# Gate and up weights of 26 experts by one 8 MB transfer each, in place of two of 4 MB

## The chip, the core and the metric

The kernel runs on one core of one Trainium2 chip. The metric is the device time of one execution in microseconds (us). The version before takes 1148.26 us (median of 3 runs, 1148.26 to 1148.38). One of its executions was profiled; the profile gives times in us from the span's start. TensorE (PE) does the matmuls, VectorE (DVE), ScalarE (ACT) and GpSimd (POOL) the rest, and SyncE (SP) issues nearly all transfers.

## The reference

One encoder layer for 256 tokens of width 1024: a token mixer, cross-attention into 256 memory tokens, then a routed feed-forward part with 32 experts. The last part is what the change touches:

```
logits = x2 @ w_router + b_router            # 256 x 32; each token takes its top 4 experts
gates  = softmax(top_vals)
h = x2[tok] @ w_gu[e] + b_gu[e]              # w_gu[e]: 1024 x 2048 f32, 8 MB: gate half, up half
g = min(h[:, :1024], 7);  u = clip(h[:, 1024:], -7, 7)
y = (u + 1) * (g * sigmoid(1.702 * g))
y @ w_down[e] + b_down[e]                    # w_down[e]: 1024 x 1024 f32, 4 MB
out = sum of gate * y over the token's 4 experts, then x <- LayerNorm(alpha * x + out)
```

Every token chooses its own experts, so every expert has some tokens, and all 32 x 12 MB of weights are read once.

## The kernel before

**Order of the experts.** The router counts the tokens of each expert. Experts are processed one after another in an order that the program computes (RANK_AT interleaves experts with many and with few tokens). I number them by this order: place 0 to place 31. A turn (UNROLL = 2) is an even place and the odd one behind it; there are 16 turns (LOOPS).

**Passes.** A pass handles up to 32 tokens (SLOTS) of one expert: gate and up in four chunks of 2 MB (64 matmuls on PE, line 1005), the scatter of the pass before (L981), transposes, the gather of the next tokens (L968), and down in two chunks (32 matmuls, L1030). An expert with more than 32 tokens takes several passes over the same weights. Places 1 and 25 are run by `two_passes`, which uses each chunk for two passes in turn, so that its four passes are two double ones; all others are run by `expert_pass`.

**Slots and transfers.** The weights lie in `ring`, 12 slots of 2 MB (16 KB in each of 128 partitions). Each of the two experts of a turn has six slots, in three units of two adjacent slots: unit 0 holds chunks 0 and 1 of gate and up, unit 1 chunks 2 and 3, unit 2 down. `load_later` runs on SP: for each unit it waits on `chunk_used` until PE has used both chunks for the last time, then issues one 4 MB transfer for the expert two places on. So place n + 2 is loaded while PE is at places n and n + 1, and the load of place n + 2's first unit is issued in the last pass of place n. All weights go through one queue in order. Places 0 to 3 are loaded in pieces of 2 MB, and so is most of place 31.

**What PE waits for.** In `expert_pass`, `chunk(c)` waits at every even chunk for the semaphores of its unit (`slot_landed`, `unit_landed`): at chunk 0 for unit 0, at chunk 2 for unit 1, and at the first chunk of down for unit 2.

Of the kernel before, what the change touches and what calls it, by code (L numbers as in the profile page):

```python
# [13 lines left out]
P = 128  # L14


D = 1024
# [15 lines left out]
N_EXP = 32  # L33
# [38 lines left out]
FILL_ORDER = [(0, 2), (0, 0), (0, 1), (0, 4), (0, 5), (0, 3), (1, 1), (1, 2), (1, 0), (1, 4), (1, 5), (1, 3)]  # L72

# [14 lines left out]
def layer_program(nc, x, memT, x_kv, w_mq, w_in, conv_p, early, early_par, late, w_out, ln_p, ln2_cols, w_cq, w_ck, w_cv, w_co,  # L88
                  w_router, b_router, w_gu, b_gu, w_down, b_down, out):
    with ExitStack() as ctx:  # L90
# [34 lines left out]
        lnp = S11[:, half:SLOT]  # L125
        ln3p = S6[:, 0:2 * D]
        normal_rows, rstd_last = S6[:, 2 * D:3 * D], S6[:, 3 * D:3 * D + P]
        aqT = qbuf[:, 0:1024].rearrange("p (m t) -> p m t", m=4)
# [278 lines left out]
        def _(sp):  # L407
# [22 lines left out]
            def load_piece_of_expert(e, c):  # L430
                src = w_gu[e, c // 2] if c < 4 else w_down[e]
                landed = unit_landed[e * UNITS_PER_EXPERT + c // 2] if c % 2 else slot_landed[chunk_slot(e, c)]
                sp.dma_start(slot_words(chunk_slot(e, c)), src[:, (c % 2) * SLOT:(c % 2) * SLOT + SLOT]).then_inc(landed, 16)

            def load_unit(e, u, i):
                at = UNIT_SLOT[u * UNITS_PER_EXPERT + i] * SLOT
                src = w_gu[bass.ds(e, 1), i].rearrange("o p n -> (o p) n") if i < 2 else w_down[bass.ds(e, 1)].rearrange("o p n -> (o p) n")
# [26 lines left out]
            def load_last_pieces(e, i, used):  # L464
                at = UNIT_SLOT[UNITS_PER_EXPERT + i]
                src = w_gu[bass.ds(e, 1), i].rearrange("o p n -> (o p) n") if i < 2 else w_down[bass.ds(e, 1)].rearrange("o p n -> (o p) n")
# [12 lines left out]
            def load_later(e0, ending=False):  # L479
# [12 lines left out]

            def load_in_pieces(e, u, i, used):
                at = UNIT_SLOT[u * UNITS_PER_EXPERT + i]
                src = w_gu[bass.ds(e, 1), i].rearrange("o p n -> (o p) n") if i < 2 else w_down[bass.ds(e, 1)].rearrange("o p n -> (o p) n")
                for h in range(2):
# [105 lines left out]
        def _(pe):  # L602
# [441 lines left out]

            def expert_pass(it, u, loads, ending=False, opening=False):
                j = pe.snap(passes, min_val=0, max_val=MAX_PASSES)

                def chunk(c):
                    s = chunk_slot(u, c)
                    if ending and c >= 2:  # L1050
                        if c % 2 == 0:
                            pe.wait_ge(slot_landed[s], 16 * (front_loads[s] + 3))
                        else:
                            pe.wait_ge(unit_landed[u * UNITS_PER_EXPERT + c // 2], it * 16 + 16)
                        return slot_words(s)
                    if c % 2 == 0:
                        pe.wait_ge(slot_landed[s], 16 * (front_loads[s] + loads))
                        pe.wait_ge(unit_landed[u * UNITS_PER_EXPERT + c // 2], it * 16 + 16)
                    return slot_words(s)
# [50 lines left out]

            def two_passes(it, u, loads):
                j = pe.snap(passes, min_val=0, max_val=MAX_PASSES)

                def chunk(c):
                    s = chunk_slot(u, c)
                    if c % 2 == 0:
                        pe.wait_ge(slot_landed[s], 16 * (front_loads[s] + loads))
                        pe.wait_ge(unit_landed[u * UNITS_PER_EXPERT + c // 2], it * 16 + 16)
                    return slot_words(s)
# [55 lines left out]

            def all_passes(it, u, ending=False):
                with pe.Fori(0, passes_at(bass.ds(it * UNROLL + u, 1))):
                    expert_pass(it, u, 2, ending)

# [5 lines left out]
            heavy_turn = HEAVY_AT // UNROLL  # L1185
            with pe.Fori(1, heavy_turn) as it:
                for u in range(UNROLL):
                    all_passes(it, u)
            for u in range(UNROLL):
                if u == HEAVY_AT % UNROLL:  # L1190
                    with pe.Fori(0, passes_at(slice(HEAVY_AT, HEAVY_AT + 1), 2), 2):
                        two_passes(heavy_turn, u, 2)
                else:
                    all_passes(heavy_turn, u)
            with pe.Fori(heavy_turn + 1, LOOPS - 2) as it:
                for u in range(UNROLL):
                    all_passes(it, u)
            pe.wait_ge(shift_landed, 16 * GROUPS)
# [3 lines left out]
            for u in range(UNROLL):  # L1202
                all_passes(LOOPS - 2, u)
            for u in range(UNROLL):
                if u == UNROLL - 1:
                    for t in range(TT):
                        for d in range(2):
                            add_rows(t, d)
                all_passes(LOOPS - 1, u, ending=u == UNROLL - 1)
            total = pe.snap(passes, min_val=1, max_val=MAX_PASSES)  # L1210
# [971 lines left out]
```

## Time and profile before

| | |
|---|---|
| median of 3 runs | 1148.26 us |
| the profiled execution | 1146.75 us, span 1144.8 us |
| PE busy | 1059.2 us (93% of the span) |
| DVE, ACT, POOL busy | 442.3, 153.9, 59.9 us |
| moved | 444.87 MB, mean 389 GB/s |
| transfers of 4 MB | 55 of gate and up, 27 of down |

PE is shown busy for 93% of the span, but a matmul counts as busy at half clock too, and between the experts PE also has waits for weights. The digits of part 2 of the page give the state in 40 equal slices of 28.6 us. The first 240 us are the mixer and the attention, the experts run from 247 us on, and the last 12 us are the final normalisation and the stores.

### The profile page before, as it was taken

The page shows a single profiled execution, that of the slowest core. Times are in us where ns is not written, and L with a number is a line of the kernel's source. Part 1 is how long each engine was busy: PE and PEld are TensorE (multiplying, and loading weights), DVE is VectorE, ACT ScalarE, POOL GpSimd, SP SyncE. Part 2 cuts the span into 40 slices and gives each one's busy share as a digit, 9 for nine tenths or more (in the row PEclk, how much of TensorE's full clock was granted, in tenths as well). Part 3 has the DMA queues.
Part 4 walks back from the last instruction along what each step waited for, and adds up shares of the span by engine and source line. Part 5 has one row for each costly group of instructions (what it writes and reads, how often), then busy time and mean ns, then how long its engine had stood idle before and what let it go on. Part 6 is the DMA issues. An engine that isn't in the chain of part 4 may idle for free.

```text
span 1144.8 us, 20191 instructions
## 1 busy us (share of the span) xinstructions
PE 1059.2 (93%) x8037; PEld 465.0 (41%) x8039; DVE 442.3 (39%) x1311; ACT 153.9 (13%) x334; POOL 59.9 (5%) x38
## 2 busy tenths in 40 slices
PE   9999999998999669999976669999979989999997
PEld 8876559543333213333321213333323333343333
DVE  2767577572533213333321113333313323333324
ACT  2142111230111001111100001111101101111101
POOL 0503370000000000000000000000000000000000
PEclk9999999999999889999987879999999999999999
DMA  9965356989999999999999999999999999999996
GB/s 331 365 233 184 110 189 253 379 324 428 423 433 428 437 430 432 432 429 434 428 437 430 432 433 428 434 428 437 429 433 434 427 433 426 436 428 429 433 425 248
DMA packets 36105, 444.87 MB, mean 389 GB/s; under 512 B 3876, under 2 KB 5160, under 8 KB 21256
## 3 DMA queue, kind: packets, MB, share of 16 engines
q1 hardware_dynamic: 33320, 439.86, 91.2%
q10 hardware_dynamic: 2752, 4.54, 1.3%
q8 instruction: 25, 0.41, 0.1%
q14 instruction: 8, 0.07, 0.0%
HBM read 443.34 MB, written 1.05 MB: 388 GB/s over the span
## 4 chain that ended last, share of the span: by engine, by line
PE 70%; DMA 23%; DVE 3%; another core or an unknown queue 2%; ACT 1%; issue 1%; DVEq 0%; SPq 0%; POOL 0%; POOLq 0%
PE bank L1005 23%; DMA ring<-in_w_down 15%; PE bank L1030 13%; DMA ring<-in_w_gu 8%; PE bank L689 6%; PE bank L981 6%; PE bank L635 5%; PE bank L968 3%; PE bank L814 2%; PE bank L877 2%; PE bank L974 2%; PE bank L1012 1%; PE bank L1018 1%; PE bank L1023 1%; PE bank L999 1%
## 5 line engine op out<-in xcount | busy, mean ns | idle before, releaser
L1005 PE MATMUL bank<-ring,wk 128*32 128x512 f32 x3072 | 369.9, 632 | 63.4 <-DMA ring<-in_w_gu 63.3
L1005 PEld LDWEIGHTS bank<-ring,wk 128*32 128x32 f32 x3072 | 103.9, 116 | 302.4 <-issue 263.8
L1030 PE MATMUL bank<-ring,wk 128*32 128x512 f32 x1632 | 204.8, 600 | 6.2 <-DMA ring<-in_w_down 6.2
L2036 DVE TENSOR_SCALAR wk<-bank 128x256 f32<-128x256 f32 x51 | 21.6, 423 | 461.3 <-PE bank L1005 460.5
L981 PE MATMUL bank<-wk 64*128 64x512 f32 x416 | 103.3, 615 | 2.9 <-ACT wk L1436 2.9
L1030 PEld LDWEIGHTS bank<-ring,wk 128*32 128x32 f32 x1632 | 62.8, 110 | 74.7 <-issue 46.8
L1424 ACT ACTIVATE wk<-wk 128x256 f32<-128x256 f32 x51 | 21.2, 417 | 455.0 <-DVE wk L2036 455.0
L635 PE MATMUL bank<-ring 128*128 128x256 f32 x320 | 70.7, 381 | 0.0
L689 PE MATMUL bank<-ring 128*128 128x512 f32 x152 | 66.4, 593 | 0.0
L981 PEld LDWEIGHTS bank<-wk 64*128 64x128 f32 x416 | 35.8, 186 | 71.4 <-issue 64.0
L635 PEld LDWEIGHTS bank<-ring 128*128 128x128 f32 x320 | 60.2, 190 | 8.9 <-issue 0.8
L968 PE MATMUL bank<-res,wk 128*32 128x256 f32 x832 | 55.7, 385 | 1.5 <-DVE wk L1986 1.4
L1436 ACT ACTIVATE wk<-bank 128x512 f32<-128x512 f32 x51 | 30.4, 597 | 190.5 <-PE bank L1030 190.2
L1894 DVE TENSOR_TENSOR wk<-bank,sm 128x256 f32<-128x256 f32 x49 | 20.8, 424 | 66.7 <-PE bank L974 66.7
L689 PEld LDWEIGHTS bank<-ring 128*128 128x128 f32 x152 | 28.6, 190 | 34.3 <-issue 34.1
L2045 DVE COPY wk<-bank 128x256 f32<-128x256 f32 x51 | 21.7, 425 | 37.4 <-PE bank L1018 37.4
L1993 DVE TENSOR_REDUCE wk<-wk 128x32 f32<-128x128 f32 x104 | 34.5, 373 | 1.8
L974 PEld LDWEIGHTS bank<-late_c,wk 128*128 128x128 f32 x104 | 16.4, 206 | 43.2 <-issue 41.9
L1986 DVE TENSOR_REDUCE wk<-wk 128x32 f32<-128x128 f32 x102 | 33.4, 369 | 0.0
L1428 ACT ACTIVATE wk<-bank 128x256 f32<-128x256 f32 x51 | 19.6, 383 | 90.7 <-PE bank L1012 90.7
L968 PEld LDWEIGHTS bank<-res,wk 128*32 128x32 f32 x832 | 22.4, 109 | 18.5 <-DVE wk L1986 2.9
L1432 ACT ACTIVATE wk<-bank 128x256 f32<-128x256 f32 x51 | 19.5, 383 | 51.4 <-PE bank L968 51.4
(369 smaller groups left out, 881.4 us busy)
## 6 DMA issues: line engine op xcount, KB each, us to landing
ring<-in_w_gu SPq DMA_DIRECT2D x55, 4096.0 KB, 34.8
ring<-in_w_down SPq DMA_DIRECT2D x27, 4096.0 KB, 38.4
ring<-in_w_gu SPq DMA_DIRECT2D x18, 2048.0 KB, 13.4
ring<-in_w_down SPq DMA_DIRECT2D x9, 2048.0 KB, 11.8
ring<-in_w_in SPq DMA_DIRECT2D x4, 2048.0 KB, 19.3
ring<-in_w_ck SPq DMA_DIRECT2D x2, 2048.0 KB, 21.7
ring<-in_w_cv SPq DMA_DIRECT2D x2, 2048.0 KB, 18.0
ring<-in_w_cq SPq DMA_DIRECT2D x2, 2048.0 KB, 8.3
```

The costliest lines, as they stand in the source:

```text
L635: ins = mm(banks[m // 2][:, (m % 2) * 256:(m % 2) * 256 + 256], cols, rhs[:, k, :], start=k == 0, stop=k == KT - 1)
L689: ins = mm(bank[:], rows[:, k, :], cols[:, k, :], start=fresh and k == 0, stop=k == KT // 2 - 1, skip_group_check=True)
L814: ins = mm(bank[:, m * P:(m + 1) * P], cols[:, k, m * P:(m + 1) * P], rows[:, k, :], start=fresh and m == 0 and k == 0, stop=k == KT // 2 ...
L877: ins = mm(bank[:], rows[k], cols[:, k, :], start=fresh and k == 0, stop=k == KT // 2 - 1, skip_group_check=True)
L968: ins = mm(strip(6, g)[:, 0:Q], hot[:, t, :], res[:, t, Q * g:Q * g + Q], start=t == 0, stop=t == 1, skip_group_check=True)
L974: ins = nc.tensor.transpose(psum[5][:, b * P:(b + 1) * P], xrows.rearrange("p (q b) -> p b q", b=2)[:, b, :], ident)
L981: ins = mm(psum[2 * t + d][:], scatT[r, t * P:(t + 1) * P], ysb[r, :], start=False, stop=end, skip_group_check=True)
L1005: ins = mm(hidden(bank, g), rows[:, kk, c, :], half_columns(w[:, kk, :], g), start=False, stop=2 * c + kk == KT - 1, skip_group_check=True)
L1030: ins = mm(strip(7, 2 * d + b), actT[:, b, 2 * c + gg, :], wd[:, gg, b, 512 * d:512 * d + 512], start=c == 0 and gg == 0 and b == 1, stop= ...
L1436: af(ysb, psum[7][:], ACT.Copy).then_inc(y_ready, 1)
L1986: ins = v.reduce_sum(hot[:, t, :], eq[:, t].rearrange("p k s -> p s k"), AX_X)
L1993: ins = v.reduce_sum(hotg1[:, t, :], eq[:, t].rearrange("p k s -> p s k"), AX_X)
```

## The change

- The gate and up weights of one expert now lie in DRAM with 64 KB in one row per partition, where there were two blocks of 32 KB per partition, and the four slots of an expert's gate and up are adjacent (for even places unit 0 and unit 1 change slots: 4 to 7, where unit 0 had 6 and 7 and unit 1 had 4 and 5).
- For places 4 to 29 (turns 2 to 14, WHOLE_TURNS) SP waits until all four chunks of gate and up are used, and issues one transfer of 8 MB. Down still goes by one of 4 MB.
- PE waits at chunk 0 of these places for the 8 MB, and no longer at chunk 2. Places 0 to 3, 30 and 31 keep their smaller transfers.
- The last turn's counts of unit 1's semaphore start 13 lower (`after`), since that semaphore isn't used in whole turns, and turn 1 of PE is written out ahead of the loop.

```
+WHOLE_TURNS = range(2, LOOPS - 1)
-UNIT_SLOT = [6, 4, 0, 8, 10, 2]
+UNIT_SLOT = [4, 6, 0, 8, 10, 2]
...
+            def load_whole_gate_and_up(e, u, used):
+                at = UNIT_SLOT[u * UNITS_PER_EXPERT] * SLOT
+                for c in range(4):
+                    sp.wait_ge(chunk_used[c], used)
+                sp.nop(nofuse=True)
+                sp.dma_start(ring[:, at:at + 4 * SLOT], w_gu[bass.ds(e, 1)].rearrange("o p n -> (o p) n")).then_inc(unit_landed[u * UNITS_PER_EXPERT], 16)
...
                 for u in range(UNROLL):
-                    for i in range(UNITS_PER_EXPERT):
+                    if whole:
+                        load_whole_gate_and_up(experts[u], u, passes_till[u])
+                    for i in range(2 if whole else 0, UNITS_PER_EXPERT):
...
             with sp.Fori(2, LOOPS - 1) as it:
-                load_later(it * UNROLL)
+                load_later(it * UNROLL, whole=True)
...
-                    if c % 2 == 0:
+                    if c % 2 == 0 and not (whole and c == 2):
                         pe.wait_ge(slot_landed[s], 16 * (front_loads[s] + loads))
-                        pe.wait_ge(unit_landed[u * UNITS_PER_EXPERT + c // 2], it * 16 + 16)
+                        pe.wait_ge(unit_landed[u * UNITS_PER_EXPERT + c // 2], own * 16 + 16)
```

On SP, the loop over turns 2 to 14, for the even place of a turn, before:

```order
L482 TENSOR_LOAD wk
L482 ISA x2
L438 ISA [waits chunk_used0,chunk_used1]
L438 DMA ring<-in_w_gu 128x8192
L438 ISA [waits chunk_used2,chunk_used3]
L438 DMA ring<-in_w_gu 128x8192
L438 ISA [waits chunk_used4,chunk_used5]
L438 DMA ring<-in_w_down 128x8192
```

and after the change:

```order
L491 TENSOR_LOAD wk
L491 ISA x2
L447 ISA [waits chunk_used3,chunk_used2,chunk_used0,chunk_used1]
L447 DMA ring<-in_w_gu 128x16384
L440 ISA [waits chunk_used4,chunk_used5]
L440 DMA ring<-in_w_down 128x8192
```

The first transfer of gate and up moves from behind the use of chunk 1 to behind the use of chunk 3.

On PE, the double pass of place 25 (`two_passes`), from the first chunk of gate and up to the end of the fourth; unit_landed3 and unit_landed4 are its units 0 and 1. Before:

```order
L1005 MATMUL bank<-ring,wk 32x512 [waits unit_landed3,slot_landed8]
L1005 MATMUL bank<-ring,wk 32x512 x7
...
L1005 MATMUL bank<-ring,sm 32x512 [waits xg_ready]
L1005 MATMUL bank<-ring,sm 32x512 x7
...
L1005 MATMUL bank<-ring,wk 32x512 x8
L1005 MATMUL bank<-ring,sm 32x512 x8
L1005 MATMUL bank<-ring,wk 32x512 [waits unit_landed4,slot_landed10]
L1005 MATMUL bank<-ring,wk 32x512 x7
```

and after:

```order
L1016 MATMUL bank<-ring,wk 32x512 [waits unit_landed3,slot_landed8]
L1016 MATMUL bank<-ring,wk 32x512 x7
...
L1016 MATMUL bank<-ring,sm 32x512 [waits xg_ready]
L1016 MATMUL bank<-ring,sm 32x512 x7
...
L1016 MATMUL bank<-ring,wk 32x512 x8
L1016 MATMUL bank<-ring,sm 32x512 x8
```

The order of the matmuls stays. The wait for the second half of the weights is gone from the third chunk, and unit_landed3, ahead of the first, now stands for all four chunks.

## Rows read from the trace of the kernel before

**Rows 1.** Page, part 2: DMA share in tenths and GB/s in 40 slices.

```profile
DMA  9965356989999999999999999999999999999996
GB/s 331 365 233 184 110 189 253 379 324 428 423 433 428 437 430 432 432 429 434 428 437 430 432 433 428 434 428 437 429 433 434 427 433 426 436 428 429 433 425 248
```

**Rows 2.** Waits of PE: line, waited for, us in total, times, longest.

```profile
PE bank L1005 <- DMA ring<-in_w_gu: 63.3, 17, 5.2
PE bank L1030 <- DMA ring<-in_w_down: 6.2, 9, 1.0
```

**Rows 3.** Chain of waits, gate and up in places 7, 9, 16, 22: start, us, what.

```profile
419.61 5.34 PE bank L1005 x32
...
433.75 6.87 PE bank L1005 x64
...
478.23 6.87 PE bank L1005 x64
...
493.05 6.87 PE bank L1005 x64
...
695.99 6.87 PE bank L1005 x64
...
870.83 6.87 PE bank L1005 x64
```

**Rows 4.** Timeline of SP: first issue's start, us to the second's end.

```profile
452.23 3.77 SPq L438 DMA_DIRECT2D ring<-in_w_gu  x2
...
511.54 3.77 SPq L438 DMA_DIRECT2D ring<-in_w_gu  x2
...
803.42 3.77 SPq L438 DMA_DIRECT2D ring<-in_w_gu  x2
...
889.33 3.76 SPq L438 DMA_DIRECT2D ring<-in_w_gu  x2
...
977.72 7.20 SPq L438 DMA_DIRECT2D ring<-in_w_gu  x2
```

**Rows 5.** Landing of in_w_down issued at 404.62, 478.25, 770.13, 844.27, 930.13, in turn.

```profile
DMA to landing us min/median/max: 53.7/53.7/53.7
...
DMA to landing us min/median/max: 38.4/38.4/38.4
...
DMA to landing us min/median/max: 37.9/37.9/37.9
...
DMA to landing us min/median/max: 51.1/51.1/51.1
...
DMA to landing us min/median/max: 54.2/54.2/54.2
```

**Rows 6.** Timeline of PE: start, us, engine, line, operation, idle before and releaser.

```profile
380.67 6.53 PE L1005 MATMUL bank<-ring,wk 128*32 128x512 f32 x32 [4.68 <-DMA ring<-in_w_gu]
...
390.47 5.04 PE L1005 MATMUL bank<-ring,wk 128*32 128x512 f32 x32 [3.28 <-DMA ring<-in_w_gu]
...
681.85 6.12 PE L1005 MATMUL bank<-ring,wk 128*32 128x512 f32 x32 [3.90 <-DMA ring<-in_w_gu]
...
856.69 5.34 PE L1005 MATMUL bank<-ring,wk 128*32 128x512 f32 x32 [4.46 <-DMA ring<-in_w_gu]
...
934.38 1.92 PE L1005 MATMUL bank<-ring,wk 128*32 128x512 f32 x16 [2.94 <-DMA ring<-in_w_gu]
...
953.80 3.64 PE L1030 MATMUL bank<-ring,wk 128*32 128x512 f32 x32 [0.20 <-DMA ring<-in_w_down]
...
1130.27 1.07 PE L1030 MATMUL bank<-ring,wk 128*32 128x512 f32 x8 [1.03 <-DMA ring<-in_w_down]
```

**Rows 7.** Landings: in_w_gu issued at 1080.49 (4 MB), in_w_down at 1089.39 (2 MB).

```profile
DMA to landing us min/median/max: 30.1/30.1/30.1
...
DMA to landing us min/median/max: 35.9/35.9/35.9
```

**Rows 8.** Page, part 6: issues, KB each, median us to landing.

```profile
out<-res SPq DMA_DIRECT2D x2, 256.0 KB, 2.4
```

More of the change, by code:

```diff
@@ L430, in load_piece_of_expert @@
             def load_piece_of_expert(e, c):
-                src = w_gu[e, c // 2] if c < 4 else w_down[e]
+                src = w_gu[e, :, (c // 2) * 2 * SLOT:(c // 2) * 2 * SLOT + 2 * SLOT] if c < 4 else w_down[e]
                 landed = unit_landed[e * UNITS_PER_EXPERT + c // 2] if c % 2 else slot_landed[chunk_slot(e, c)]
@@ L465, in load_last_pieces @@
                 at = UNIT_SLOT[UNITS_PER_EXPERT + i]
-                src = w_gu[bass.ds(e, 1), i].rearrange("o p n -> (o p) n") if i < 2 else w_down[bass.ds(e, 1)].rearrange("o p n -> (o p) n")
+                src = w_gu[bass.ds(e, 1)].rearrange("o p n -> (o p) n")[:, i * 2 * SLOT:i * 2 * SLOT + 2 * SLOT] if i < 2 else w_down[bass.ds(e, 1)].rearrange("o p n -> (o p) n")
                 sp.wait_ge(chunk_used[2 * i], used)
@@ L477, in load_last_pieces, with load_later @@
                     sp.dma_start(slot_words(at + 1)[:, half:SLOT], src[:, SLOT + half:2 * SLOT]).then_inc(done, 16)
-            def load_later(e0, ending=False):
+            def load_later(e0, ending=False, whole=False):
                 passes_till = [sp.value_load(cum_i[0:1, bass.ds(e0 + (u - UNROLL), 1)], min_val=1, max_val=MAX_PASSES) for u in range(UNROLL)]
@@ L494, in load_in_pieces @@
                 at = UNIT_SLOT[u * UNITS_PER_EXPERT + i]
-                src = w_gu[bass.ds(e, 1), i].rearrange("o p n -> (o p) n") if i < 2 else w_down[bass.ds(e, 1)].rearrange("o p n -> (o p) n")
+                src = w_gu[bass.ds(e, 1)].rearrange("o p n -> (o p) n")[:, i * 2 * SLOT:i * 2 * SLOT + 2 * SLOT] if i < 2 else w_down[bass.ds(e, 1)].rearrange("o p n -> (o p) n")
                 for h in range(2):
@@ L1043, in _, with expert_pass @@
             open_sum(1, 1)
-            def expert_pass(it, u, loads, ending=False, opening=False):
+            def expert_pass(it, u, loads, ending=False, opening=False, whole=False, after=0):
                 j = pe.snap(passes, min_val=0, max_val=MAX_PASSES)
@@ L1049, in chunk @@
                     s = chunk_slot(u, c)
+                    own = it - after if c // 2 == 1 else it
                     if ending and c >= 2:
@@ L1109, in expert_pass, with two_passes @@
                 pe.reg_add(passes, passes, 1)
-            def two_passes(it, u, loads):
+            def two_passes(it, u, loads, whole=False, after=0):
                 j = pe.snap(passes, min_val=0, max_val=MAX_PASSES)
@@ L1115, in chunk @@
                     s = chunk_slot(u, c)
-                    if c % 2 == 0:
+                    if c % 2 == 0 and not (whole and c == 2):
+                        own = it - after if c == 2 else it
                         pe.wait_ge(slot_landed[s], 16 * (front_loads[s] + loads))
-                        pe.wait_ge(unit_landed[u * UNITS_PER_EXPERT + c // 2], it * 16 + 16)
+                        pe.wait_ge(unit_landed[u * UNITS_PER_EXPERT + c // 2], own * 16 + 16)
                     return slot_words(s)
@@ L1174, in passes_at, with all_passes @@
                 return pe.value_load(npass_i[0:1, place], min_val=least, max_val=SEQ // SLOTS)
-            def all_passes(it, u, ending=False):
+            def all_passes(it, u, ending=False, whole=False, after=0):
                 with pe.Fori(0, passes_at(bass.ds(it * UNROLL + u, 1))):
-                    expert_pass(it, u, 2, ending)
+                    expert_pass(it, u, 2, ending, whole=whole, after=after)
             with pe.Fori(0, passes_of_first):
@@ L1185, in _ @@
             heavy_turn = HEAVY_AT // UNROLL
-            with pe.Fori(1, heavy_turn) as it:
+            for u in range(UNROLL):
+                all_passes(1, u)
+            with pe.Fori(2, heavy_turn) as it:
                 for u in range(UNROLL):
-                    all_passes(it, u)
+                    all_passes(it, u, whole=True)
             for u in range(UNROLL):
@@ L1191, in _ @@
                     with pe.Fori(0, passes_at(slice(HEAVY_AT, HEAVY_AT + 1), 2), 2):
-                        two_passes(heavy_turn, u, 2)
+                        two_passes(heavy_turn, u, 2, whole=True)
                 else:
-                    all_passes(heavy_turn, u)
+                    all_passes(heavy_turn, u, whole=True)
             with pe.Fori(heavy_turn + 1, LOOPS - 2) as it:
                 for u in range(UNROLL):
-                    all_passes(it, u)
+                    all_passes(it, u, whole=True)
             pe.wait_ge(shift_landed, 16 * GROUPS)
@@ L1202, in _ @@
             for u in range(UNROLL):
-                all_passes(LOOPS - 2, u)
+                all_passes(LOOPS - 2, u, whole=True)
             for u in range(UNROLL):
@@ L1208, in _ @@
                             add_rows(t, d)
-                all_passes(LOOPS - 1, u, ending=u == UNROLL - 1)
+                all_passes(LOOPS - 1, u, ending=u == UNROLL - 1, after=len(WHOLE_TURNS))
             total = pe.snap(passes, min_val=1, max_val=MAX_PASSES)
```

13 lines of the change are left out of this document (7 added, 6 removed).

## The prediction

> **What bounds the kernel now.** I read four views, in this order. The slices of the page first [rows 1]: from the tenth on, the DMA engines show a busy share of nine tenths or more in every slice, at 423 to 437 GB/s, up to the last. The waits of PE next [rows 2]: 17 waits for gate and up weights, 63.3 us in all, 9 for down weights, 6.2 us. Both say that from about 260 us on the weight stream is the resource. Then the end: the last down piece is waited for 1.03 us, at 1130.27 [rows 6], and only the closing stage follows. So the end is the end of the stream, and the stream's end is its work plus every gap in which its queue is empty. In the kernel before there is no such gap. Last, how close it comes to one: for each expert I compare the time at which SP issues a load with the time at which the transfer ahead of it in the queue lands.
>
> Six units of 4 MB lie between the landings of two down units, 404.62 + 53.7 = 458.3 and 478.25 + 38.4 = 516.6 [rows 5]: 9.72 us each, 431 GB/s.
>
> The queue is shortest where SP has waited for an expert of three or four passes. There the first gate and up unit is issued at 452.23 (place 7), 511.54 (place 9), 803.42 (place 19), 889.33 (place 22) and 977.72 (place 25, the double one) [rows 4], and the unit ahead lands at 458.3, 516.6, 808.0, 895.4 and 984.3 [rows 5]. That leaves 6.1, 5.1, 4.6, 6.1 and 6.6 us. Everywhere else in places 4 to 29 the timeline and the landings leave clearly more, or the load isn't merged.
>
> **What the change takes from this slack.** It acts twice.
>
> *The issue comes later.* SP issues at the use of chunk 3, where it issued at that of chunk 1. That is where the second issue of each pair stands now: the pairs end 3.77 us after the first one's start (7.20 us at place 25, where every chunk serves two passes) [rows 4], so at 456.0, 515.3, 807.2, 893.1 and 984.9. On SP only the down load stands behind the wait, which is later anyway. By itself this leaves room everywhere but at place 25, where 984.9 is past 984.3.
>
> *The pass starts later.* PE now waits at chunk 0 for all 8 MB. Where it runs ahead of the stream, it starts a place when the second half lands: at 419.61 rather than 9.8 us before in place 7. The first two chunks, which were computed while the second half came in, now lie behind it. An ordinary pass takes 493.05 - 478.23 = 14.82 us from start to start [rows 3]. From 419.61 the next would start at 434.43 + e, against 433.75 now: 0.7 us + e late. Places 16 (681.85, next 695.99) and 22 (856.69, next 870.83) give the same 0.7 + e [rows 3, 6]. So most of the 9.7 us is hidden, because down used to be waited for in that pass; it lands before PE gets there now.
>
> e is the price of the clock. After waits of 3.3 to 4.7 us PE ran the next 32 matmuls in 5.04, 5.34, 6.12 and 6.53 us [rows 6] against 6.87 / 2 = 3.43 at full clock [rows 3]: 1.6, 1.9, 2.7 and 3.1 more, since the granted clock was the lower of its two levels (1.2 GHz against 2.4) for part of them. The idle time ahead of these passes will be some 12 us (29.2 us for 12 MB less a pass and e), which no row shows; I take the mean of the four, e = 2.3, between 1.6 and 3.1.
>
> At place 25 nothing hides it. There chunks 0 and 1 are used for two passes, with transposes and the scatter between, from 934.38, and the down wait of 0.20 us ends at 953.80 [rows 6], so PE needs 19.2 us from chunk 0 to down. Starting 9.72 us later, at 944.1, it reaches down at 963.3 + e: 9.5 + e late instead of 0.7 + e.
>
> *A start takes time.* After an empty queue the data doesn't flow at once. A store of 256 KB takes 2.4 us from issue to landing [rows 8], of which 0.6 are data at 431 GB/s, so start and completion together are at most 1.8. Counted from the end of the issue I take 1.2, between 0 and 1.8; it is no more than the row allows.
>
> **The gaps**, each as the end of the issue now + lateness + 1.2 - landing ahead:
> - place 7: 456.0 + 0.7 + e + 1.2 - 458.3 = e - 0.4 = 1.9 us
> - place 9: PE is still as late as after place 7 (it never waits in between), 515.3 + 0.7 + e + 1.2 - 516.6 = e + 0.6 = 2.9 us. This counts from the old stream, so it contains place 7's 1.9.
> - Behind it PE waits for weights again from place 13 on, so stream and PE are late alike.
> - place 19, lateness from place 16: 807.2 + 0.7 + e + 1.2 - 808.0 = e + 1.1 = 3.4 us
> - place 22: 893.1 + 0.7 + e + 1.2 - 895.4 = e - 0.4 = 1.9 us
> - place 25: 984.9 + 9.5 + e + 1.2 - 984.3 = e + 11.3 = 13.6 us
>
> Together 12.6 + 4e = 21.8 us. Place 28 has only the issue of place 30 behind it, which isn't merged, and PE finds its weights late by as much as the stream; nothing there. The PE waits that grow in places 5, 6 and 12 to 15 cost nothing, since the queue reaches past them.
>
> **What it gives back.** Larger transfers carry a smaller fixed share. Between the landing at 1080.49 + 30.1 = 1110.6 and that at 1089.39 + 35.9 = 1125.3 [rows 7] three pieces of 2 MB came in, 4.9 us each, or 9.8 for 4 MB against 9.72. So doubling a row's length saves about 0.08 us per pair. I take the same for the next doubling: 26 x 0.08 = 2.1 us, between 0 (if the chip cuts the 64 KB rows in two) and, for the rounding of these landings, 4. The slots' new order, the later use of slot 5 at the start, the wait instructions and the written-out turn are covered by the stream's slack: nothing.
>
> The Trainium skill, "DMA: Bandwidth & Descriptors", sections "Anatomy of one DMA" and "Rules for kernel authors", speaks for the change: a transfer costs 2.0 us and its bytes at 436 GB/s (for those issued from GpSimd), and small ones are to be coalesced. By that fit 4 MB take 11.6 us, and an estimate of 26 x 2.0 = 52 us would be given back. The trace doesn't agree: 9.72 us per 4 MB, as the next transfer already stands in the queue. By the rows the saving is 2.1.
>
> **Sum.** 21.8 - 2.1 = +19.7 us. On the profiled execution the span goes from 1144.8 to 1164.5, its time from 1146.75 to 1166.5; the median of the runs shown is 1.5 above that, so 1168.0 us.
>
> **The rivals.**
> 1. *Only the later issue counts, PE's late start is absorbed.* This ends on the other side, as no change. For it: at places 7, 16 and 22 all but 0.7 us of the 9.7 is hidden behind the down wait, if e is nothing. It would need PE to reach down at place 25 with the weights' landing too. Gaps then: place 9 516.5 - 516.6 = 0, place 19 808.4 - 808.0 = 0.4, place 25 986.1 - 984.3 = 1.8; 2.2 - 2.1 = +0.1, 1148.4 us. Against it: 19.2 us of work stand between chunk 0 and down at place 25. It turns where the lateness at place 25 is under 2 us. Chance 0.07.
> 2. *Larger transfers win.* The slack is more than I read, since a load starts the moment that it is issued and the queue never runs dry, and the fixed share goes: -2.1 us, 1146.2 (up to -4). Against: issue times on PE's side, which the rows have to a tenth. Chance 0.04.
> 3. *Only the double place makes a gap.* If the clock returns at once (e = 0) and a load starts in 0.3 us, places 7, 19 and 22 lose next to nothing and place 25 loses 11: about +9, 1157 us. Chance 0.10.
> 4. *Worse.* The clock stays low through a whole pass (e = 6.9 at the four places, 12.6 + 27.5 - 2.1): +38, 1186 us; or rows of 64 KB flow worse, at 424 rather than 431 GB/s for 218 MB: +9 more, 1177. For it: idle times of 12 us, which the trace never shows. Against: the lower clock ends within 6.5 us of work in each row. Chance 0.08.
>
> The forecast has 0.71. With e from 1.6 to 3.1, the start from 0 to 1.8 and the saving from 0 to 4 it lies between 12.6 + 6.4 - 4.8 - 4 = +10.2 and 12.6 + 12.4 + 2.4 - 0 = +27.4 us, 1158.5 and 1175.7 (the start changes four gaps). The ends that need all of them at once are unlikely, so the range 1157 to 1175 holds the forecast and half of rival 3, and leaves out rivals 1, 2 and 4. A measurement can tell 0.2%, 2.3 us, from no change: rival 2's 2.1 us stays within it, but its 4 does not, so I split its chance. Faster 0.02, same 0.09 (rival 1 and the rest of rival 2), slower 0.89.
>
> **What would show it.** The DMA share dips after places 7 or 9, 19, 22, and for over 10 us after 25; DMA idles between the issue and the unit ahead there. PE starts place 7 near 419.6 and its second pass near 436.7; the second pass pair of place 25 is some 12 us late beside the stream. PE's waits for in_w_gu are half as many but longer, and those for in_w_down go from the merged places. The rate of the full stretches stays 431 to 433 GB/s. I am wrong if the share stays full behind place 25, or if PE reaches down there no later than its weights.

## The result, and the profile after

| | before | after |
|---|---|---|
| median of 5 runs each, on one chip | 1148.26 us (1147.39 to 1149.21) | 1176.36 us (1173.58 to 1177.99) |
| profiled execution, span | 1146.75, 1144.8 us | 1175.41, 1173.6 us |
| PE busy | 1059.2 us | 1046.2 us |
| moved | 444.87 MB | 444.90 MB |

The change makes the kernel slower: 1.0243 times the time before (95% interval 1.0232 to 1.0254), 28.1 us. The forecast was 1168.0 us, with a range up to 1175. The direction and five of the six places were right; the time is 1.4 us outside the range, and 0.7 above the 1175.7 that the prediction got by adding up all its bounds.

Part 2 of the page, which answers to [rows 1] (a slice is 29.3 us now; PEclk is the granted clock in tenths):

```profile
PEclk9999999999999779999977879999979979998999
DMA  9965366799999999999999999998999998699996
GB/s 329 371 206 179 108 244 258 304 402 427 423 439 432 433 429 380 429 427 431 429 429 429 429 431 438 447 436 355 431 429 393 429 430 358 271 437 427 403 427 255
```

The stream no longer runs through. Dips stand in slice 16 (380 GB/s), 28 (355), 31 (393), 34 and 35 (358, 271) and 38 (403). Every other slice from the tenth to the 39th keeps 423 GB/s or more, as before. So the transfers aren't slower; the stream pauses. Five of the six pauses in the table below lie in these slices. The sixth, at place 9, is too short to show in its slice (the 18th, 427) and is read from the landings.

The waits of PE, which answer to [rows 2]:

```profile
PE bank L1016 <- DMA ring<-in_w_gu: 111.2, 10, 13.9
```

Ten waits instead of 17, but 111.2 us instead of 63.3, and none for down (6.2 us before).

The gaps, as in the prediction, are read from three things: SP's issues [rows 4], the landing of the down unit ahead [rows 5], and the landing of the load itself. SP's timeline:

```profile
459.35 0.33 SPq L447 DMA_DIRECT2D ring<-in_w_gu  x1
...
518.66 0.33 SPq L447 DMA_DIRECT2D ring<-in_w_gu  x1
...
814.35 0.33 SPq L447 DMA_DIRECT2D ring<-in_w_gu  x1
...
903.93 0.33 SPq L447 DMA_DIRECT2D ring<-in_w_gu  x1
...
1008.01 0.33 SPq L447 DMA_DIRECT2D ring<-in_w_gu  x1
...
1096.81 3.77 SPq L440 DMA_DIRECT2D ring<-in_w_gu  x2
```

From issue to landing of the down units ahead of them, issued at 407.47, 481.86, 777.54, 851.63, 941.28 and 1051.23:

```profile
DMA to landing us min/median/max: 51.4/51.4/51.4
...
DMA to landing us min/median/max: 38.0/38.0/38.0
...
DMA to landing us min/median/max: 34.4/34.4/34.4
...
DMA to landing us min/median/max: 52.6/52.6/52.6
...
DMA to landing us min/median/max: 53.6/53.6/53.6
...
DMA to landing us min/median/max: 47.8/47.8/47.8
```

And from issue to landing of the loads themselves (the last line is the pair of 4 MB for place 30, its first the minimum):

```profile
DMA to landing us min/median/max: 21.8/21.8/21.8
...
DMA to landing us min/median/max: 22.0/22.0/22.0
...
DMA to landing us min/median/max: 22.1/22.1/22.1
...
DMA to landing us min/median/max: 21.9/21.9/21.9
...
DMA to landing us min/median/max: 23.0/23.0/23.0
...
DMA to landing us min/median/max: 12.8/15.9/19.0
```

Where the queue is full, 8 MB take 19.35 us from landing to landing and 4 MB 9.71 (medians; a few loads land later, the one issued at 911.57 by 1.2 us). What the distance of two landings has beyond that is lost. A place stands for the load that is issued when PE has used that place's weights. Times in us:

| place | down ahead lands | issue ends, beyond that: forecast, measured | start: forecast, measured | lost: forecast, measured |
|---|---|---|---|---|
| 7 | 458.9 | 0.7, 0.8 | 1.2, 2.1 | 1.9, 2.9 |
| 9 | 519.9 | -0.2, -0.9 | 1.2, 2.3 | 1.0, 1.4 |
| 19 | 811.9 | 2.2, 2.8 | 1.2, 2.4 | 3.4, 5.2 |
| 22 | 904.2 | 0.7, 0.0 | 1.2, 2.2 | 1.9, 2.3 |
| 25 | 994.9 | 12.4, 13.4 | 1.2, 3.3 | 13.6, 16.8 |
| 28 | 1099.0 | none, -1.9 | none, 2.8 | 0, 0.9 |
| sum | | 15.8, 16.2 (places 7 to 25) | 6.0, 12.3 | 21.8, 29.5 |

(Place 9's forecast is what it adds to place 7's. The sums are of unrounded values. The start is the lost time less the column before it: for place 19, 814.35 + 22.1 = 836.45, less 811.9 is 24.55; less 19.35 it is 5.2, of which 2.8 are the late issue.) The lateness of the issues came out almost as forecast, 16.2 against 15.8. What is off is the start: 12.3 us against 6.0.

PE's timeline, gate and up of places 6, 7, 16, 22, 25 (the number in brackets is the idle time ahead, with its releaser):

```profile
391.06 8.43 PE L1016 MATMUL bank<-ring,wk 128*32 128x512 f32 x64 [13.58 <-DMA ring<-in_w_gu]
...
420.12 9.25 PE L1016 MATMUL bank<-ring,wk 128*32 128x512 f32 x64 [12.68 <-DMA ring<-in_w_gu]
...
686.00 9.43 PE L1016 MATMUL bank<-ring,wk 128*32 128x512 f32 x64 [12.50 <-DMA ring<-in_w_gu]
...
865.54 8.41 PE L1016 MATMUL bank<-ring,wk 128*32 128x512 f32 x64 [13.92 <-DMA ring<-in_w_gu]
...
956.18 3.64 PE L1016 MATMUL bank<-ring,wk 128*32 128x512 f32 x16 [13.60 <-DMA ring<-in_w_gu]
...
977.02 3.71 PE L1041 MATMUL bank<-ring,wk 128*32 128x512 f32 x32
```

The place starts when the whole 8 MB are in. In place 25 the down piece is reached 20.8 us after chunk 0 and waits for nothing: it landed long before.

### The profile page after: what moved, and what is told of

It is laid out like the page before. It is cut to its first block, busy times and chain, and to the rows that moved or that the text cites. A ratio compares the mean times of both kernels' runs of the same rounds, so it can differ in the third digit from the quotient of the medians.

```text
span 1173.6 us, 20065 instructions
## 1 busy us (share of the span) xinstructions
PE 1046.2 (89%) x8037; PEld 463.9 (40%) x8039; DVE 442.8 (38%) x1311; ACT 154.2 (13%) x334; POOL 60.1 (5%) x38
## 2 busy tenths in 40 slices
DMA packets 32363, 444.90 MB, mean 379 GB/s; under 512 B 3460, under 2 KB 4744, under 8 KB 20840
## 4 chain that ended last, share of the span: by engine, by line
PE 72%; DMA 22%; DVE 3%; another core or an unknown queue 1%; ACT 1%; issue 1%; DVEq 0%; SPq 0%; POOL 0%; POOLq 0%
PE bank L1016 26%; DMA ring<-in_w_gu 22%; PE bank L1041 11%; PE bank L700 6%; PE bank L992 6%; PE bank L646 5%; PE bank L979 3%; PE bank L825 2%; PE bank L888 2%; PE bank L985 1%; PE bank L1023 1%; PE bank L1029 1%; PE bank L1034 1%; PE bank L1010 1%; PE bank L856 1%
## 5 line engine op out<-in xcount | busy, mean ns | idle before, releaser
L1016 PE MATMUL bank<-ring,wk 128*32 128x512 f32 x3072 | 358.2, 617 | 111.2 <-DMA ring<-in_w_gu 111.2
L1041 PE MATMUL bank<-ring,wk 128*32 128x512 f32 x1632 | 206.0, 599 | 0.0
L1909 DVE TENSOR_TENSOR wk<-bank,sm 128x256 f32<-128x256 f32 x49 | 20.8, 425 | 60.0 <-PE bank L985 59.9
L1443 ACT ACTIVATE wk<-bank 128x256 f32<-128x256 f32 x51 | 19.6, 384 | 103.1 <-PE bank L1023 103.1
L985 PE MATMUL bank<-late_c,wk 128*128 128x128 f32 x104 | 26.4, 336 | 0.0
```

The costliest lines, as they stand in the source:

```text
L985: ins = nc.tensor.transpose(psum[5][:, b * P:(b + 1) * P], xrows.rearrange("p (q b) -> p b q", b=2)[:, b, :], ident)
L1016: ins = mm(hidden(bank, g), rows[:, kk, c, :], half_columns(w[:, kk, :], g), start=False, stop=2 * c + kk == KT - 1, skip_group_check=True)
L1041: ins = mm(strip(7, 2 * d + b), actT[:, b, 2 * c + gg, :], wd[:, gg, b, 512 * d:512 * d + 512], start=c == 0 and gg == 0 and b == 1, stop= ...
```

## The experiments

All ratios are to the kernel before, run on the same chip in the same session. "Lost" is worked out as above, or as a stretch's length times one less its rate over that of before.

**The two halves of the change.** `x1_start_late`: loads as before the change, but PE waits at chunk 0 for both halves. So it has the late start alone.

```
             with sp.Fori(2, LOOPS - 1) as it:
-                load_later(it * UNROLL, whole=True)
+                load_later(it * UNROLL)
...
+                        if whole and c == 0:
+                            pe.wait_ge(unit_landed[u * UNITS_PER_EXPERT + 1], own * 16 + 16)
```

> Loads as before: two transfers of 4 MB, each issued as soon as its own two chunks are used. Only PE changes: in places 4 to 29 it waits at chunk 0 for both halves. THEORY (late start times late issue, and a load into an empty queue costs 2.4 us between the end of its issue and its data rather than the 1.2 I had taken, 3.0 at place 25): gaps behind places 9, 19 and 25 of 0.5, 1.2 and 978.1 + 9.5 + 1.8 + 3.0 - 982.8 = 9.6 us, none behind 7 and 22; +11.3, 1159.6 us. RIVAL A (only the later issue matters): within 1 us of before, 1148 to 1149. RIVAL B (the rows of 64 KB are what makes the empty queue dear, start cost 1.2): place 25 alone, +8, 1156.

Measured: 1163.40 us (1161.59 to 1164.52), ratio 1.0124 (1.0107 to 1.0140): +15.3. Both rivals are out; my own number is 3.8 short. By the landings, places 7, 9, 19, 22 and 25 lost 2.0, 0.9, 1.3, 0.0 and 8.2 us, and the down load behind place 25, issued at 1016.52, another 3.5. I had expected nothing at place 7 nor at that down load.

`x2_issue_late`: SP waits for all four chunks and then issues two loads of 4 MB; PE waits for each half as before. So it has the late issue alone.

```
                 for c in range(4):
                     sp.wait_ge(chunk_used[c], used)
                 sp.nop(nofuse=True)
-                sp.dma_start(ring[:, at:at + 4 * SLOT], w_gu[bass.ds(e, 1)].rearrange("o p n -> (o p) n")).then_inc(unit_landed[u * UNITS_PER_EXPERT], 16)
+                for i in range(2):
+                    load_unit(e, u, i)
...
-                    if c % 2 == 0 and not (whole and c == 2):
+                    if c % 2 == 0:
```

> SP waits for all four chunks of gate and up in places 4 to 29 and then issues two transfers of 4 MB; PE waits for each half as before. THEORY: issue ends at 456.0, 515.3, 807.2, 893.1 and 984.9, plus 2.4 to 3.0 us of start, against landings at 458.3, 516.6, 808.0, 895.4 and 984.3 (982.8 without the slip of one engine): gaps 0.1, 1.1, 1.6, 0.1 and 3.6 to 5; +6.4, 1154.7 us. RIVAL A (only the later issue matters): the whole loss, 1174 to 1178. RIVAL B (start cost 1.2 with rows of 32 KB): +2 to 3, 1151.

Measured: 1161.13 us (1160.21 to 1162.70), ratio 1.0114 (1.0097 to 1.0131): +13.0. This is 6.4 more than I expected, and meets neither rival. By the landings, places 7, 9, 19, 22 and 25 lost 1.0, 2.4, 1.2, 2.5 and 4.9 us, where I had expected 0.1, 1.1, 1.6, 0.1 and 3.6 to 5. The excess is largest at places 9 and 22, though the issue there ended 2.1 and 2.2 us before the load ahead landed.

`x3_both_4mb`: both edits together, still two loads of 4 MB with rows of 32 KB. So it is the change without its large transfer.

> Late issue and late start as in the changed kernel, but by two transfers of 4 MB with rows of 32 KB. THEORY (nothing hangs on the size but 0.07 us per pair): the changed kernel's time plus 26 x 0.07 = 1.9, 1178.2 us. RIVAL A says the same of this run. RIVAL B (64 KB rows make the start dear): about 1.2 us less in each of five gaps, 1171 to 1173 us.

Measured: 1177.85 us (1176.72 to 1178.52), ratio 1.0253 (1.0236 to 1.0270): +29.7, as expected by the theory; rival B's 1171 to 1173 is out. The halves alone cost 15.3 + 13.0 = 28.3, nearly as much, but by the landings that is in part chance. At place 25 the issue ended 6.3 us before the load ahead landed in the kernel before, and 6.2, 3.0 and 13.4 us behind it in x1, x2 and x3: 12.4, 9.3 and 19.7 us later. The losses there are 8.2, 4.9 and 15.5 us, in each case 4.2 to 4.4 less. So place 25 had some 4.2 us of slack, and each half alone already used all of it: together they cost more than their sum there, and at place 19 too (4.7 against 1.3 and 1.2). What makes up for it is the down load on which x1 lost 3.5 us and x3 nothing, and place 9, where x3 lost 1.0 behind a larger gap at place 7.

x1, x2 and x3 keep the changed kernel's layout of the weights in DRAM and its order of slots; so does x8 (below), which comes out 1.8 us from the kernel before. So neither is the cause. The large transfer itself gives back 1.5 us (the intervals overlap), where I had forecast 2.1; by the landings it is 26 x (2 x 9.71 - 19.35) = 1.8.

The stretch behind place 25 shows both halves. Windows of the changed kernel, x3, x1, x2 and x4 (below), in this order; columns: stretch, length, busy us of PE, PEld, DVE, ACT, POOL with counts, granted clock, DMA share, GB/s:

```profile
990.00:1012.00 22.00, 21.02 (x184) 7.12 (x180) 5.36 (x20) 1.19 (x3) 0.00 (x0) 1.00 0.26 100
```

```profile
990.00:1012.00 22.00, 21.02 (x192) 7.17 (x188) 4.55 (x17) 1.78 (x4) 0.00 (x0) 1.00 0.26 101
```

```profile
990.00:1012.00 22.00, 20.48 (x174) 7.45 (x178) 7.28 (x25) 2.19 (x5) 0.00 (x0) 1.00 0.69 286
```

```profile
990.00:1012.00 22.00, 20.48 (x184) 7.67 (x180) 10.15 (x37) 2.80 (x6) 0.00 (x0) 1.00 0.80 332
```

```profile
990.00:1012.00 22.00, 20.48 (x185) 7.66 (x180) 10.16 (x37) 2.79 (x6) 0.00 (x0) 1.00 1.00 430
```

Against 431 GB/s, 22 x (1 - 100 / 431) = 16.9 us are lost with the change, 16.8 in x3, 7.4 with the late start alone and 5.1 with the late issue alone, and nothing in x4. PE is busy nearly all the time in all five: here DMA waits for PE, not PE for DMA.

**The double place.** `x4_units_in_12_13`: turns 12 and 13 (places 24 to 27) go by units as before, all other turns as changed.

```
-WHOLE_TURNS = range(2, LOOPS - 1)
+WHOLE_TURNS = (2, 3, 4, 5, 6, 7, 8, 9, 10, 11, 14)
```

> The changed kernel, but turns 12 and 13 (places 24 to 27) by units of 4 MB, issued and waited for as before. THEORY (the loss sits in single gaps, the largest behind place 25): the gap of 16.7 us behind place 25 goes, and so does the 2.3 behind place 22, whose successor's load is issued 3.4 us earlier: 1176.4 - 19.0 = 1157.4 us. RIVAL (each merged place costs its share): 4 of 26 shares, -4.3, 1172 us.

Measured: 1158.61 us (1157.90 to 1160.45), ratio 1.0092 (1.0073 to 1.0111). Back come 17.8 us. By the landings nothing is lost any more at places 22, 25 and 28, where the changed kernel lost 2.3, 16.8 and 0.9, and 2.9, 1.1 and 5.1 us still are at places 7, 9 and 19. The theory is met and the rival's 1172 is out.

`x8_merged_where_queue_is_long`: whole transfers only in turns 2, 6, 7 and 9, where the queue is longest.

```
-WHOLE_TURNS = range(2, LOOPS - 1)
+WHOLE_TURNS = (2, 6, 7, 9)
```

> Merged in turns 2, 6, 7 and 9 alone (places 4, 5, 12 to 15, 18, 19), where the queue reaches at least 10 us past the issue and no long expert starts late. THEORY: no gap, 8 x 0.07 us of fixed cost saved: 0.6 us under before, not to be told from it (1147.6). RIVAL (each merged place costs its share of 28 us): +8.6, 1157 us.

Measured in 10 runs: 1150.48 us (1148.76 to 1153.15) against 1148.71, ratio 1.0016 (1.0003 to 1.0028). So the large transfer has no use of its own even where it does no harm. The gaps are gone, as expected, but the small gain isn't there; why it is 1.8 us slower rather than 0.6 faster stays open. (In its profiled execution single loads landed 0.1 to 1.0 us late with the queue full, 4.6 us in all, against 1.5 before. The trace doesn't tell what held them up.)

**The clock.** `x11_clock_kept_up`: ahead of places 7, 16, 22 and 25 PE does 40 matmuls on data that nobody uses, while it would be idle.

```
+            def warm_up():
+                pe.wait_ge(xg_ready, pe.snap(passes, min_val=0, max_val=MAX_PASSES) + 1)
+                keep_warm(20)
...
+                            if UNROLL * first + u in WARM_AHEAD:
+                                warm_up()
                             all_passes(first, u, whole=whole, after=whole_before(first))
```

> The changed kernel, with 20 idle matmuls (some 10 us) ahead of the wait for weights at places 7, 16, 22 and 25, so that the clock doesn't fall there. THEORY (the lower clock in the first pass is part of PE's lateness, and each us of it is a us of gap): e of 2.2, 2.4, 1.4 and 1.8 us goes at these places: -7.8, 1168.6 us. RIVAL C (the clock is beside the path, the gaps come from the waits alone): within 1 us of the changed kernel, 1175 to 1177.

Measured: 1181.32 us (1180.05 to 1182.76), ratio 1.0282 (1.0264 to 1.0301). It tells nothing on the price of the clock, since the clock wasn't held. PE's timeline, idle matmuls (L932) and place 7:

```profile
410.36 8.90 PE L932 MATMUL bank<-late_c 128*128 128x256 f32 x40
...
421.83 8.77 PE L1037 MATMUL bank<-ring,wk 128*32 128x512 f32 x64 [2.25 <-DMA ring<-in_w_gu]
```

2.25 us of idle time were left behind them (up to 5.19 at place 22), and the pass took 8.77 us, where 7.05 is usual at the higher clock. A wait of 2.25 us doesn't always cost it: in the kernel before, the 16 matmuls at 934.38 took 1.92 us, full speed, after 2.94 us [rows 6]. The kernel became 5 us slower than the changed one; by the landings 3.4 of them are in the gaps, and why stays open.

`x12_clock_kept_up_longer`: the same with 24, 25, 31 and 28 in the call for the four places.

> As x11, where the idle matmuls ended 2.3 to 5.2 us before the weights and the clock fell all the same: now 24, 25, 31 and 28 of them, which should end within 1 us of the landing at places 7, 16, 22 and 25. THEORY (the lower clock at the start of those passes is part of PE's lateness): first passes of 7.05 us instead of 8.4 to 9.4, 7.8 us less in the gaps, 1168.6 us. RIVAL C (the clock is beside the path): 1175 to 1177.

Measured: 1172.10 us (1170.58 to 1175.05), ratio 1.0206 (1.0184 to 1.0228). PE's timeline, the first matmuls of places 7, 16, 22 and 25:

```profile
422.30 8.77 PE L1037 MATMUL bank<-ring,wk 128*32 128x512 f32 x64 [2.88 <-DMA ring<-in_w_gu]
...
689.04 7.08 PE L1037 MATMUL bank<-ring,wk 128*32 128x512 f32 x64 [0.27 <-DMA ring<-in_w_gu]
...
866.52 7.07 PE L1037 MATMUL bank<-ring,wk 128*32 128x512 f32 x64 [0.23 <-DMA ring<-in_w_gu]
...
956.31 1.92 PE L1037 MATMUL bank<-ring,wk 128*32 128x512 f32 x16 [0.78 <-DMA ring<-in_w_gu]
```

The clock was held at three of four places. There the passes are 9.43 - 7.08 = 2.4, 8.41 - 7.07 = 1.3 and 3.64 - 1.92 = 1.7 us shorter, 5.4 in all, and the kernel is 4.3 us faster than the changed one. That is 3.5 less than the 7.8 expected, in part since place 7 kept its slow pass. The granted clock of the first matmuls of places 16 and 25 with the change (same columns as above; 1.00 is 2.4 GHz, 0.50 is 1.2 GHz):

```profile
686.10:695.40 9.30, 9.30 (x66) 2.20 (x66) 0.00 (x0) 0.00 (x0) 0.00 (x0) 0.75 1.14 493
...
956.30:959.80 3.50, 3.50 (x17) 0.58 (x16) 0.00 (x0) 0.00 (x0) 0.00 (x0) 0.50 1.02 440
```

and in x12:

```profile
689.10:696.10 7.00, 7.00 (x66) 2.35 (x66) 0.00 (x0) 0.00 (x0) 0.00 (x0) 1.00 0.94 400
...
956.40:958.20 1.80, 1.80 (x17) 0.41 (x16) 0.00 (x0) 0.00 (x0) 0.00 (x0) 1.00 1.18 510
```

The issues show that it matters for the stream. Against the landing of the load ahead, those of places 19, 22 and 25 ended 3.1, 2.1 and 2.0 us earlier than in the changed kernel (0.3 and 2.1 us before it and 11.4 behind it). So the price of the clock is on the path that sets the end, as the prediction's e had it; rival C is out.

**The start, measured by itself.** `x9_alone_4mb`: the kernel before, but SP issues each 4 MB load only once the one ahead has landed, in turns 2 to 14 (78 loads).

```
                         sp.wait_ge(chunk_used[2 * i + 1], passes_till[u])
+                        if turn is not None:
+                            ahead = (u * UNITS_PER_EXPERT + i - 1) % len(unit_landed)
+                            sp.wait_ge(unit_landed[ahead], turn * 16 + (16 if u or i else 0))
                         sp.nop(nofuse=True)
                         load_unit(experts[u], u, i)
```

> The kernel before, but in turns 2 to 14 SP issues each of the 78 units of 4 MB only once the unit ahead has landed, so every one goes into an empty queue. It measures what such a start costs. THEORY (2.4 to 3.0 us from the end of the issue to the data, plus the issue's 0.33 and some 0.1 to see the landing): 78 x 2.8 to 3.4 = +220 to +265 us, 1368 to 1413. AS PREDICTED FIRST (1.2 us): 78 x 1.6 = +127, 1275 us.

Measured: 1372.35 us (1370.53 to 1374.18), ratio 1.1950 (1.1919 to 1.1980). That is 224 / 78 = 2.9 us per load, against 1.2 in the prediction, which would have given about 1275. `x9_alone_8mb` does the same with the changed kernel's 52 loads (26 of 8 MB, 26 of 4 MB).

```
                 for c in range(4):
                     sp.wait_ge(chunk_used[c], used)
+                sp.wait_ge(unit_landed[UNITS_PER_EXPERT - 1 if u else 2 * UNITS_PER_EXPERT - 1], turn * 16 + (16 if u else 0))
...
+                        if whole:
+                            sp.wait_ge(unit_landed[u * UNITS_PER_EXPERT], turn * 16 + 16)
```

> The changed kernel, each of the 52 transfers of turns 2 to 14 (26 of 8 MB, 26 of 4 MB) issued only once the one ahead has landed. THEORY (the start costs the same for 8 MB in rows of 64 KB as for 4 MB, 2.87 us by x9_alone_4mb): 52 x 2.87 = 149 us over before, less 1.9: 1295 us, and somewhat more where PE is late besides. RIVAL B (large rows make the start dearer, 4 us and more): 26 x 1.1 on top, 1325 and over.

Measured: 1303.88 us (1303.56 to 1304.21), ratio 1.1354 (1.1331 to 1.1376): 156 / 52 = 3.0 us per load, much the same as with 4 MB; the theory's 1295 is 9 us short, and the rival's 1325 and more is out. SP's timeline of the 4 MB kernel, and its page, part 6:

```profile
402.83 0.33 SPq L438 DMA_DIRECT2D ring<-in_w_gu  x1
415.15 0.33 SPq L438 DMA_DIRECT2D ring<-in_w_down  x1
...
ring<-in_w_gu SPq DMA_DIRECT2D x55, 4096.0 KB, 12.2
ring<-in_w_down SPq DMA_DIRECT2D x27, 4096.0 KB, 12.2
```

and of the 8 MB kernel, with the landing of the load issued at 421.69:

```profile
421.69 0.33 SPq L448 DMA_DIRECT2D ring<-in_w_gu  x1
443.75 0.33 SPq L440 DMA_DIRECT2D ring<-in_w_down  x1
...
DMA to landing us min/median/max: 21.8/21.8/21.8
```

A lone load lands 12.2 us (4 MB) or 21.8 us (8 MB) after its issue began, and in a full queue they take 9.71 and 19.35: 2.5 us more in both. 0.33 of it is the issue itself; the other 2.2 are what I had called the start. Four of the five merged places of the changed kernel show the same, 2.1 to 2.4 us. Most of the rest of the 2.9 is SP's answer: its next issue began 0.3 us after the landing.

The trace holds 16 semaphore events for the landing of each load, as many as there are DMA engines, and the landing is the last of them. This divides the start. Counted from the end of the issue, and less 9.71 or 19.35, the first event came after 1.6 us in the two x9 runs (median), and after 1.5 to 1.6 us at all six places of the table. The last came 0.6 us behind it in x9, 0.5 to 0.8 at places 7, 9, 19 and 22, 1.7 at place 25 and 1.2 at place 28. So the time to the first engine's landing is the same everywhere, and the difference is how far the last engine is behind.

The Trainium skill, "DMA: Bandwidth & Descriptors", section "Anatomy of one DMA", puts a fixed 2.0 us on a transfer that GpSimd issues, beside its bytes at 436 GB/s. By an estimate from that fit these two loads, which SyncE issues, would take 11.6 and 21.2 us, against 12.2 and 21.8 measured: 0.6 short, when the queue is empty. With another load queued, the trace doesn't show the fixed part at all (9.71 us). The prediction set the figure only against what merging gives back, where it doesn't hold, and not against the gaps, where it comes near.

**How early is early enough.** `x13a_margin_5us` and `x13b_margin_3us`: the kernel before, but each load waits for a signal that GpSimd gives a number of dummy instructions after the landing of the load two ahead. So the queue holds one load, and the next comes a set time before it ends. The edit of x13a is shown; x13b has 33 in place of 24.

```
                         sp.wait_ge(chunk_used[2 * i + 1], passes_till[u])
+                        if turn is not None:
+                            sp.wait_ge(may_load, 6 * (turn - 2) + 3 * u + i + 1)
...
+            for n in range(6 * (LOOPS - 3)):
+                turn, ahead = 2 + n // 6, n % 6 - 2
+                pool.wait_ge(unit_landed[ahead % 6], turn * 16 + (16 if ahead >= 0 else 0))
+                for i in range(24):
+                    link(nc.gpsimd.memset(convp[:], 0.0))
+                nc.gpsimd.memset(convp[:], 0.0).then_inc(may_load, 1)
+                pool.wait_ge(may_load, n + 1)
```

> The kernel before, but each of the 78 units of 4 MB in turns 2 to 14 is issued some 5 us after the unit two ahead has landed, so some 5 us before the queue runs empty (GpSimd spends the time on idle memsets). THEORY (a start takes 2.4 to 3.0 us, so 5 us suffice): within 3 us of before, 1148 to 1152. RIVAL D (a queue this short already costs, since the 16 engines are 2 to 3.5 us apart): 1 us per unit, 1225.

> The same with some 3 us before the queue runs empty. THEORY as I had it (a gap only where start is over the margin): 0 to 0.3 us per unit, 1148 to 1172. RIVAL D (x1 and x2 lost 1 to 2.6 us on the slowest engine in places with 2 to 3 us left): 78 x 1 to 2, 1226 to 1304.

Measured: x13a 1158.04 us (1157.42 to 1158.65), ratio 1.0084 (1.0063 to 1.0104); x13b 1221.55 us (1221.04 to 1222.06), ratio 1.0637 (1.0615 to 1.0658). Windows of x13a and x13b over 500 us:

```profile
400.00:900.00 500.00, 442.23 (x3676) 152.83 (x3672) 146.39 (x528) 49.26 (x111) 167.80 (x1275) 0.93 1.00 428
```

```profile
400.00:900.00 500.00, 415.18 (x3404) 140.72 (x3400) 137.40 (x494) 46.35 (x104) 211.47 (x1596) 0.92 0.97 395
```

and, for the same stretch, the loads with their count and the median from issue to landing, of x13a:

```profile
ring<-in_w_gu SPq DMA_DIRECT2D x34, 4096.0 KB, 14.4
```

and of x13b:

```profile
ring<-in_w_gu SPq DMA_DIRECT2D x32, 4096.0 KB, 14.7
```

From the end of an issue to the landing of the load ahead it was 4.3 us in x13a (median of the 51 loads of this stretch; 4.0 to 5.0) and 3.5 in x13b (of 47; 2.6 to 5.5). In x13a a load loses 9.9 / 78 = 0.13 us, in x13b 73 / 78 = 0.94. Both theories failed: x13a is 6 us above its 1152 (its rival's 1225 is far out), and x13b is 50 us above its 1172, with the lower end of rival D, 1226, nearly met.

What separates the two is the margin of the first engine to finish the load ahead: in x13a it was 1.9 us or more in every load, in x13b the median was 1.3, and 70% of the loads had less than 1.6. With 1.5 to 1.6 us from issue to the first engine's landing, no engine of x13a had to wait for an issue, and in x13b most of the first ones did. That fits the order of the two, but not the amount: by an estimate from these margins the first engine waits 0.4 us per load in x13b, and 0.94 are lost. The rest stays open. Nor is it a sharp threshold in the landing: loads that were issued 3.4 us (x1) and 3.5 us (x4) before the one ahead landed lost nothing.

## Why the prediction was right or wrong

*What bounds the kernel: right.* Outside the gaps the rate is the same, and the lost times add up to the loss: 29.5 lost less 1.8 saved is 27.7, against 28.7 of the profiled executions. Of the last 1.0, 0.8 stand ahead of the first gap: the down load of place 4 landed at 315.56 + 26.2 = 341.8 before and at 315.85 + 26.7 = 342.6 after. The prediction had put the slots' new order at the start at nothing; whether that is the cause isn't shown.

*Where the gaps open: right for five of six.* Places 7, 9, 19, 22 and 25 are the ones forecast, and place 25 makes more than half. I had place 28 with nothing. The load for place 30 isn't merged, but its issue depends on a place that starts late, and it ended only 1.9 us before the landing ahead: 0.9 us lost. That term was put at nothing, on the ground that PE would be late by no more than the stream.

*How late the issues are: right.* 16.2 us in sum against 15.8, in part by luck: place 9 is 0.7 less than forecast, since the gap of place 7 ahead of it came out larger, and the other four are 1.1 more together. This holds the absorbed 9.7 us, the later chunk and e. e was 2.2, 2.4, 1.3 and 1.7 us against 2.3 forecast, and x12 shows that it is paid.

*"A start takes time": this step failed.* The prediction took 1.2 us from the end of the issue, "between 0 and 1.8; it is no more than the row allows". Measured alone it is 2.2, and in the table 2.1 to 2.4, 3.3 at place 25: together 6.3 us of the 8.9 by which the profiled time was missed (1175.41 against 1166.5). The bound was wrong, not only the value in it. It came from a store of 256 KB [rows 8], another direction and another size, and I treated the row nearest at hand as if it enclosed a 4 MB load. 1.8 us does enclose the time to the first engine's landing (1.5 to 1.6), but not that to the last one's, which is what PE and the end wait for.

The trace of the kernel before held a better row. Its DMA engines were idle when the 2 MB load at 233.56 was issued (the first row is of SP, the second a window with the columns as above, the third the landing):

```profile
233.56 4.64 SPq L433 DMA_DIRECT2D ring<-in_w_down  x2
...
233.00:234.00 1.00, 1.00 (x8) 0.71 (x7) 0.86 (x5) 0.00 (x0) 0.00 (x0) 1.00 0.00 0
...
DMA to landing us min/median/max: 7.4/7.4/7.4
```

Less the 4.9 us of 2 MB in a full queue [rows 7] and the 0.3 of the issue, that is 2.2 us, the value that the runs showed.

With 2.2 the prediction's own sum, in which the start counts in four gaps, gives 25.8 - 2.1 = +23.7, about 1172 and in the range. What carries it out of the range is 1.1 more of start at place 25, 0.9 at place 28, 1.1 more of lateness at places 7, 19, 22 and 25, and the 0.8 ahead of the first gap. The 1.1 at place 25 is the last engine's, 1.7 us behind the first rather than 0.5 to 0.8. It doesn't belong to the place: in x3 the last engine was 0.6 behind there, and the start 2.1. What held the engine up isn't shown.

*The slack was read too large.* I let a load be in time if its issue ended 1.2 us before the landing ahead. x2, with the late issue alone, cost 13.0 us, where its expectation, which already took 2.4 to 3.0 us for the start, had 6.4. So a longer start alone doesn't explain it. In x1 and x2 the issue of six loads ended 1.1 to 3.3 us before the load ahead landed, and in these the last engine landed 1.7 to 2.9 us behind the first, against 0.4 to 0.6 in the four whose issue came later than that. So a load that comes just in time for the last engine isn't safe. Why one engine falls behind then isn't shown.

*The two halves.* The late start (+15.3) and the late issue (+13.0) cost about the same, where I had left the issue room "everywhere but at place 25". At place 25 either one alone uses up the slack.

*What it gives back: right.* 1.5 to 1.8 us against 2.1; the rows of 64 KB flow no worse.

*The rivals.* 1 and 2 are dead by the time. 3 is out: it gives place 25 11 us, which lost 16.8, and next to nothing to the others, which lost 11.8 together. 4 is dead: after 12 to 14 us of idle time a pass took 8.4 to 9.5 us, not the 13.7 (twice 6.87 [rows 3]) of a pass wholly at the lower clock, and the rate stayed. That its other branch, slower rows of 64 KB, gives 1177 is chance: x3 takes 1177.85 with rows of 32 KB.

## What to carry to other kernels

When one transfer stream is the bound, merging two of its loads saves almost nothing, since a queued load's fixed cost is hidden already; and it makes the issue wait for the last of all the buffers it fills, and the consumer for the last of all the bytes. What counts is how long before the landing of the load ahead the next is issued: here about 4.3 us were nearly enough (0.13 us lost per load), and at about 3.5, scattered from 2.6 to 5.5, 0.94 were lost. By these runs a merge is safe only where more than some 4 us remain after both delays. The place to look at first is the one at which the most work stands between the first use of a buffer and the last, here the double pass. Price a start by a load of the same direction into an empty queue (here the trace before had one, of 2 MB), and if there is none, keep the upper bound open.

## What the runs showed of the hardware

- A load from DRAM that SyncE issues into an empty queue takes 2.5 us from the start of its issue beyond its time in a full queue, the same for 2 MB (7.4 against 4.9), 4 MB (12.2 against 9.71) and 8 MB (21.8 against 19.35).
- In a full queue the same loads show 0.07 us of fixed share per 8 MB (2 x 9.71 - 19.35).
- Its 16 semaphore events lie apart. The first comes 1.5 to 1.6 us after the issue's end beyond the time in a full queue, the last mostly 0.4 to 0.8 us later. In a full queue the distance of first and last stays as it is, 1.9 to 3.4 us in the kernel before, and costs nothing.
- With a margin of 4.3 us (4.0 to 5.0) from the issue's end to the landing ahead a 4 MB load lost 0.13 us, with 3.5 (2.6 to 5.5) 0.94.
- After 12.5 to 13.9 us of idle time 64 matmuls of 128x512 took 8.41 to 9.43 us (places 6, 7, 16, 22), against 7.08 where idle matmuls had run until 0.27 us before. 2.25 us of idle time behind idle matmuls were already enough to lose the higher clock (8.77 us at place 7 of x11), and 2.94 us at place 25 of the kernel before were not.
